# A decoder step on one Trainium2 core: the second feed-forward's gate/up tiles as seven block products in place of eight

## The reference

```
h = x + 1/2 * SwiGLU(RMSNorm(x))                    (feed-forward 1, D_FF = 2816)
n = RMSNorm(h); P = n @ w_in                        (u, q, k, v, index q/k/w, two gates)
h = h + (sigmoid(gs) * S5(u) + sigmoid(ga) * DSA(q, k, v)) @ w_out
h = h + 1/2 * SwiGLU(RMSNorm(h))                    (feed-forward 2)
y = RMSNorm(h)

def _swiglu(x, w_in, w_out):
    gate, up = jnp.split(x @ w_in, 2, axis=-1)
    return (jax.nn.silu(gate) * up) @ w_out
```

## Time and profile before

| | us |
|---|---|
| runs of the kernel before | 1451.26, 1454.88, 1445.98; median 1451.26 |
| the profiled execution, its span | 1450.0 |
| PE busy | 1376.6 (95%) |
| DVE, ACT, POOL busy | 654.6, 495.6, 265.2 |
| feed-forward 1, about | 24 to 430 |
| mixer, about | 432 to 1033 |
| feed-forward 2 and the end, about | 1033 to 1450 |

### The profile page before, as it was taken

One profiled execution on the slowest core, in us unless ns is written; L12 is line 12 of the kernel. 1 busy time (PEld: TensorE's weight loads), 2 busy tenths in 40 slices (PEclk: granted clock), 3 DMA queues, 4 the chain that ended last, 5 costly groups with the idle time before them and its releaser, 6 DMA issues.

```text
span 1450.0 us, 28752 instructions
## 1 busy us (share of the span) xinstructions
PE 1376.6 (95%) x11422; PEld 1289.9 (89%) x11422; DVE 654.6 (45%) x1093; ACT 495.6 (34%) x720; POOL 265.2 (18%) x325
## 2 busy tenths in 40 slices
PE   6999999999999899997999888899999999999996
PEld 5999999999987678875999777689999999999996
DVE  4333333434352226975987423245533443343344
ACT  5332222212232221244877432332432222222234
POOL 4000000288205002022667422100000000000000
PEclk9999999999997999999999999999999999999998
DMA  9522232333234363234222669663233322233221
GB/s 135 154 82 87 80 89 87 90 90 89 66 108 67 81 88 98 49 109 77 73 59 85 216 213 348 200 209 88 73 102 87 87 88 87 87 87 88 80 66 62
DMA packets 228818, 152.62 MB, mean 105 GB/s; under 512 B 27425, under 2 KB 209833, under 8 KB 228730
## 3 DMA queue, kind: packets, MB, share of 16 engines
q1 hardware_dynamic: 200512, 121.07, 28.9%
q0 software_dynamic: 7728, 19.97, 5.6%
q10 hardware_dynamic: 20490, 10.36, 3.3%
HBM read 141.85 MB, written 8.34 MB: 104 GB/s over the span
## 4 chain that ended last, share of the span: by engine, by line
PE 90%; DVE 3%; ACT 3%; issue 2%; DMA 1%; SPq 1%; ACTq 0%; DVEq 0%
PE ps L642 58%; PE ps L622 9%; PE ps L1036 3%; PE ps L1052 3%; PE ps L1153 3%; PE ps L1122 2%; PE ps L1205 1%; DVE uv L2139 1%; PE ps L1184 1%; PE ps L819 1%; PE ps L1067 1%; PE ps L926 1%; PE ps L1076 1%; PE ps L922 1%; PE ps L807 0%
## 5 line engine op out<-in xcount | busy, mean ns | idle before, releaser
L1778 DVE TENSOR_TENSOR w_low<-wraw,w_high 128x1024 fp32r<-128x1024 f32 x144 | 179.5, 1247 | 319.1 <-ACT w_high L1268 319.1
L1268 ACT ACTIVATE w_high<-wraw 128x1024 fp32r<-128x1024 f32 x144 | 152.6, 1060 | 443.3 <-PE ps L642 438.8
L642 PE MATMUL ps<-hn_high,w_high 128*128 128x272 f32 x1408 | 292.1, 289 | 2.9 <-DVE w_low L1778 2.9
L642 PE MATMUL ps<-hn_high,w_low 128*128 128x272 f32 x1408 | 291.9, 289 | 0.0
L642 PE MATMUL ps<-hn_low,w_high 128*128 128x272 f32 x1408 | 290.7, 288 | 0.0
L642 PEld LDWEIGHTS ps<-hn_high,w_high 128*128 128x128 f32 x1408 | 222.2, 189 | 3.1 <-issue 3.0
L642 PEld LDWEIGHTS ps<-hn_low,w_high 128*128 128x128 f32 x1408 | 221.8, 189 | 0.0
L642 PEld LDWEIGHTS ps<-hn_high,w_low 128*128 128x128 f32 x1408 | 220.2, 189 | 0.0
L642 PE MATMUL ps<-act_high,w_high 128*128 128x272 f32 x832 | 173.1, 289 | 3.4 <-DVE act_low L1778 1.9
L642 PE MATMUL ps<-act_high,w_low 128*128 128x272 f32 x832 | 172.0, 288 | 0.0
L642 PE MATMUL ps<-act_low,w_high 128*128 128x272 f32 x832 | 171.7, 288 | 0.0
(11 more groups left out here) (364 smaller groups left out, 1801.0 us busy)
## 6 DMA issues: line engine op xcount, KB each, us to landing
wraw<-in_w_ffn_in SPq DMA_DIRECT2D x88, 512.0 KB, 3.9
wraw<-in_w_ffn_out SPq DMA_DIRECT2D x32, 512.0 KB, 3.8
wslot<-in_w_in SPq DMA_DIRECT2D x16, 512.0 KB, 3.8
wraw<-in_w_ffn_out SPq DMA_DIRECT2D x16, 384.0 KB, 3.4
wslot<-in_w_in SPq DMA_DIRECT2D x4, 1024.0 KB, 5.6
wslot<-in_w_s_glu SPq DMA_DIRECT2D x16, 256.0 KB, 3.0
biasmem<-in_cache_k SPq DMA_DIRECT2D x16, 256.0 KB, 4.4
biasmem<-in_cache_k POOLq DMA_DIRECT2D x16, 256.0 KB, 5.1
```

Source lines behind the costliest of these rows:

```text
L642: ins = pe.matmul(ps[:, bank + h, 0:HALF], a[:, w_at, k, :], x[:, lo_at(k) if x is x_lo else k, h * HALF:(h + 1) * HALF], start=(k == 0 an ...
L1268: act_e.activation(wh[:, j % 2, :, :], wraw[:, j, :, :], ACT.Copy).then_inc(s["hi_done"], 1)
L1778: return dve.tensor_tensor(o, a, b, op)
```

## The change

For hidden tile f, write the gate tile's weights as two blocks of 512 input rows, G0 and G1, the up tile's as L0 and L1 ("lift"), and the scaled activations as X with upper and lower 512 channels and left and right token halves. Gate and up for both halves are 4 results of 2 blocks each, 8 block products. The change forms them from 7 products (the Winograd form of Strassen's scheme), each of 4 blocks x 3 pairs x one half = 12 matmuls, 84 a tile:

- **Weight sums.** Four of the seven left operands are sums of the blocks: L0+L1, L0+L1+G0, G0+L0, L0+L1+G0+G1 (signs sit in the activations and in the combining). They are formed in a DRAM scratch scr_w by POOL: plain copies, then transfers with accum_op=add. 22 tiles x 4 sums, 4 copies and 4 accumulates each of 256 KB, in 24 rounds; in each, copies, a wait for all, accumulates, a wait for all. Rounds 0 to 10 come behind the second unit of feed-forward 1, rounds 11 to 18 hold the 17 products for the S5 matrices between their transfers, rounds 19 to 23 come behind the clearing of uch, ahead of the page loads.
- **Activations.** hn_high and hn_low are replaced by xc_high and xc_low, 7 x [128, 4, 272]: three are quarters of X, one a difference, three sums made by cross_sums on DVE. scaled, block_high, cross_high run on ACT, block_low, cross_low on DVE.
- **PE.** `product` does 12 matmuls, with both passes of the high weights first and the low weights' pass behind a wait of its own. Seven products of a tile use four banks; products 4, 5, 6 add onto banks 0, 1, 3 after these were read. Tiles alternate between two sets of banks.
- **Combining.** ACT copies bank 0 to mid; DVE forms u, v, the right half of up, the two gate halves (the right one in two steps) and the left half of up, seven operations of 272 columns, then the gating product as before.
- **Splits.** Weights are split in pairs of products: three of 1024 columns and one of 512 a tile. Raw weights alternate between wraw (odd tiles) and a new wfront (even tiles); SP loads seven pieces of 256 KB a tile, released two tiles ahead.
- SP waits for all the sums (sums_in) and for the attention's matmuls before the first loads of feed-forward 2. The squares of the norms get other places. Feed-forward 1 is as before.

```diff
+            def product(f, p, high_ready, low_ready, block_wait=None):
+                pe.wait_ge(s["hi_done"], high_ready)
+                for n in range(3):
+                    a, x = ((high_slot(p), xc_high), (high_slot(p), xc_low), (low_slot(p), xc_high))[n]
+                    if n == 2:
+                        pe.wait_ge(s["lo_done"], low_ready)
+                    for k in range(4):
+                        if block_wait is not None and n < 2:
+                            block_wait(n, k)
+                        ins = pe.matmul(bank_of(f, p), a[:, k, :], x[:, XC[p], k, :], start=(n == 0 and k == 0 and p < 4),
...
+            def fused_tile(g, f, r=None):
...
+                for p in range(7):
...
+                    if p == 4:
+                        pe.wait_ge(s["first_out"], at(f + 1, 1))
...
+                    if p == 5:
+                        pe.wait_ge(s["combined"], at(combined_at(f, "v"), 7))
+                    if p == 6:
+                        pe.wait_ge(s["combined"], at(combined_at(f, "up1"), 7))
...
+            def cross_sums(j):
+                dve.wait_ge(s["x_scaled"], X0 + j + 1)
+                if j < 4:
+                    tt(xdiff[:, j, :], side(xs_block(j), 0), side(xs_block(j), 1), ALU.subtract).then_inc(s["cross_done"], 1)
+                    return
+                c = cross(j - 4)
+                dve.wait_ge(s["cross_done"], j - 3)
+                link(tt(c[:, 0, :], side(xs_block(j), 1), xdiff[:, j - 4, :], ALU.add))
+                tt(c[:, 1, :], side(xs_block(j - 4), 1), side(xs_block(j), 1), ALU.subtract)
+                tt(c[:, 2, :], side(xs_block(j), 0), c[:, 0, :], ALU.subtract).then_inc(s["cross_done"], 1)
...
+            def combine(g, f):
+                dve.wait_ge(s["unit_done"], product_at(g, f, 2))
+                dve.wait_ge(s["first_out"], f + 1)
+                tt(mid[:, 1, :], bank_of(f, 2), mid[:, 0, :], ALU.subtract).then_inc(s["combined"], 1)
+                dve.wait_ge(s["combined"], combined_at(f, "u"))
+                tt(mid[:, 2, :], mid[:, 1, :], bank_of(f, 1), ALU.subtract).then_inc(s["combined"], 1)
...
+                    for f in range(f0, f0 + m):
+                        if f > f0:
+                            combine_up0(g, f - 1)
+                            gate2(f - 1)
+                            tile_low_pair(g, f, 2)
+                            hidden_low(f - 1, f - 1 - f0)
+                            tile_low_pair(g, f, 3)
+                        if f < f0 + m - 1:
+                            tile_low_pair(g, f + 1, 0)
...
+                        combine(g, f)
+                        combine_up1(g, f)
+                        if f < f0 + m - 1:
+                            tile_low_pair(g, f + 1, 1)
...
+                        if f == 0:
+                            root_inverse(2)
+                        combine_gate(g, f)
```

DVE behind the units of `@ w_out`:

```diff
-                scaled_low(i)
+                if i in (6, 7):
+                    tile_low_pair(0, 0, i - 4)
                 if i:
+                    cross_sums(i - 1)
+                    block_low(i - 1)
+                    if i >= 2:
+                        cross_low(i - 2)
                     add_square(2, i - 1)
+            tile_low_pair(0, 0, 0)
+            cross_sums(DK - 1)
+            block_low(DK - 1)
+            cross_low(DK - 2)
+            tile_low_pair(0, 0, 1)
+            cross_low(DK - 1)
             add_square(2, DK - 1)
```

POOL:

```diff
+            def sum_copies(c):
+                if c < FK:
+                    pool.dma_start(scr_w[0, c], lift(0, c)).then_inc(s["sums_in"], 16)
+                    pool.dma_start(scr_w[2, c], gate(0, c)).then_inc(s["sums_in"], 16)
+                if 1 <= c <= FK:
+                    pool.dma_start(scr_w[1, c - 1], scr_w[0, c - 1]).then_inc(s["sums_in"], 16)
+                if c >= 2:
+                    pool.dma_start(scr_w[3, c - 2], scr_w[1, c - 2]).then_inc(s["sums_in"], 16)
+            def sum_adds(c):
+                if c < FK:
+                    pool.dma_start(scr_w[0, c], lift(1, c), accum_op=ALU.add).then_inc(s["sums_in"], 16)
+                    pool.dma_start(scr_w[2, c], lift(0, c), accum_op=ALU.add).then_inc(s["sums_in"], 16)
...
+            pool.wait_ge(s["unit_done"], 2)
...
+            ROUNDS, EARLY, LATE = FK + 2, 11, 19
...
+            for c in range(EARLY):
+                sum_copies(c)
+                sums_landed(c, 0)
+                sum_adds(c)
+                sums_landed(c, 1)
             pool.wait_ge(s["s5_scalars"], 2)
             pool.wait_ge(s["early_act"], 1)
+            for c in range(EARLY, LATE):
+                sum_copies(c)
+                lag_product(c - EARLY, 2 * (c - EARLY))
+                sums_landed(c, 0)
+                sum_adds(c)
+                if c == EARLY:
+                    lag_product(8, 1)
+                else:
+                    step_product(c - EARLY - 1, 2 * (c - EARLY) + 1)
+                sums_landed(c, 1)
+            step_product(7, 16)
             pool.sem_inc(s["prep_done"], 1)
...
+            for c in range(LATE, ROUNDS):
+                sum_copies(c)
+                sums_landed(c, 0)
+                sum_adds(c)
+                sums_landed(c, 1)
```

More of the change, by code:

```diff
@@ L414, in ffn_plan @@
                 u, tl, g_ = u + 2 * m, tl + m, g_ + m
-                yield "out", f0, m, u, tl, FK * which + g_
+                yield "out", f0, m, u, tl, g_
                 u, tl = u + DK, tl + DK
-        def in_parts(which, f0, m):
-            if which == 0:
-                return [(i, i + 1) for i in range(m // 2)]
-            return [(0, 1), (1, m // 2)] if f0 == 0 else [(0, m // 2)]
+        U1 = FFN_UNITS + DK
+        X0 = 5
+        XC = (0, 1, 4, 5, 2, 3, 6)
+        BANK = (0, 1, 2, 3, 0, 1, 3)
@@ new lines, in f_group, with split_at, out_split_at, product_at @@
+        def f_group(f):
+            return sum(f >= f0 for f0, _ in GROUPS) - 1
+        def split_at(g, f, q):
+            if f > GROUPS[g][0]:
+                return U1 + 4 * f + DK * g + q + 1
+            if g == 0:
+                return U1 + (q + 2) % 4 + 1
+            return U1 + 4 * f + DK * g + (q + 3 if q < 2 else q - 2 - DK + 3)
+        def out_split_at(g, j):
+            return U1 + 4 * sum(GROUPS[g]) + DK * g + j + 1 + (2 if g < 2 and j >= 2 else 0)
+        def product_at(g, f, p):
+            return U1 + 7 * f + DK * g + p + 1
@@ new lines, in out_done_at, with gated_at, out_added_at, combined_at @@
+        def out_done_at(g, j):
+            return U1 + 7 * sum(GROUPS[g]) + DK * g + j + 1
+        def gated_at(f):
+            return FE0 + FFN_TILES + DK + f + DK * f_group(f) + 1
+        def out_added_at(g, j):
+            return FE0 + FFN_TILES + DK + sum(GROUPS[g]) + DK * g + j + 1
+        COMBINED = ("u", "v", "up1", "gate0", "gate1", "gate1_scaled", "up0")
+        def combined_at(f, what):
+            return 7 * f + COMBINED.index(what) + 1
+        def pair_bytes(q):
+            return 32 if q < 3 else 16
@@ L715, in ffn @@
                                     pe.wait_ge(s["ffn_ev"], i * 2 + (t0 + j // 2 + FE0 - 1))
-                                unit(j % 2, hnh, hnl, DK, 4 * (j // 2) + 2 * (j % 2), norm_block if which == 0 and f0 == 0 and j == 0 else None)
+                                unit(j % 2, hnh, hnl, DK, 4 * (j // 2) + 2 * (j % 2), norm_block if f0 == 0 and j == 0 else None)
                     else:
@@ new lines, in first_blocks, with body, out_unit2 @@
+            def first_blocks(p):
+                def body(n, k):
+                    ready = (block_at(k), cross_at(k), cross_at(k + 4), cross_at(k + 4), block_at(k + 4), block_at(k + 4), cross_at(k + 4))[p]
+                    pe.wait_ge(s["xn_low" if n else "xn_high"], ready)
+                return body
+            def out_unit2(g, f0, m, j):
+                pe.wait_ge(s["lo_done"], FE0 + out_split_at(g, j))
+                if j < 2:
+                    pe.wait_ge(s["combined"], combined_at(f0 + m - 2 + j, "up0"))
+                else:
+                    pe.wait_ge(s["out_scaled"], DK * g + j - 1)
+                hidden = last_hidden(m, FE0 + FK + f0 + m)
+                for k in range(m):
+                    if j == 0:
+                        hidden(k)
+                    for n in range(3):
+                        a, x = ((wh[:, j % 2, :, :], acth), (wh[:, j % 2, :, :], actl), (wl[:, j % 2, :, :], acth))[n]
+                        for h in range(2):
+                            ins = pe.matmul(ps[:, 4 * (j % 2) + h, 0:HALF], a[:, k, :], side(x[:, k, :], h),
+                                            start=(k == 0 and n == 0), stop=(k == m - 1 and n == 2), skip_group_check=True)
+                ins.then_inc(s["unit_done"], 1)
@@ new lines, in ffn2 @@
+            def ffn2():
+                for g, (f0, m) in enumerate(GROUPS):
+                    for f in range(f0, f0 + 2):
+                        fused_tile(g, f)
+                    with pe.Fori(1, m // 2) as r:
```

(13 more changed lines are left out.)

476 lines of the change are left out of this document (349 added, 127 removed).

## The result

The changed kernel takes 1472.95 us (median of 4 runs, 1464.93 to 1476.89), the kernel before beside it 1453.07: a ratio of 1.014, interval 1.010 to 1.018. It is slower by 1.4%, and outside the predicted range of 1421 to 1468. The profiled executions have spans of 1472.7 and 1450.0: 22.7 us to explain, and with the 33.1 us that the products were to save, 56 us of new cost.

The account below looks back on a forecast made before the run. PE was taken as the bound, busy 95% of a 1450.0 us span. 1450.0 - 33.1 (products) + 8.5 (start) + 0 (sums) + 4 (exchange) = 1429.4, with 1.3 for the median about 1430; own range 1421 to 1438, all told 1421 to 1468.

Parts of the forecast that it names:

- Products, -33.1: Second feed-forward's gate/up tiles on PE: 84 matmuls in place of 96, 22 tiles x 12 x 0.1253 us, 33.1 us gone.
- rival D: Gate/up tiles: 84 matmuls with a new moving operand each take as long as 96, no gain, 1463 us; chance 0.03.
- Steady tile, 0: Gate/up tile of 10.52 us: DVE's 8.8 us and ACT's 5.6 hide under the products, PE never waits; cost zero.
- Sums on POOL, 0: Weight-sum rounds on POOL's queue: S5 products done at 433.3, before PE needs prep_done at 436.1; cost 0.
- R = 18.5: Length in us of one POOL round of four copies and four accumulates, bounds 8.7 and 46.
- rival A: POOL's rounds take 19 to 22 us, prep_done up to 25 us late; 1447 us, range 1432 to 1455; chance 0.19.
- Start of the feed-forward, +8.5: Second feed-forward's start: PE stalls 5.5, 2.4 and about 2.1 us for DVE's work; 8.5 us lost, bounds 0 and 12.
- Exchange of u, +4: Exchange of u through DRAM, beside POOL's last five rounds, takes a fifth more: 4 us, ends 0 and 12.
- Weight loads of feed-forward 1, 0: First feed-forward's weight loads, issued three units (18 us) ahead at 33% DMA share, lose nothing beside the rounds: 0.
- The slower rival (B): POOL's rounds over 22.6 us delay prep_done; at 24 it is 61 us late, 1491 us; chance 0.16.

Follow-up runs that it names:

- e1: Changed kernel with PE's wait for an even tile's first weight pair, in the tile loop, set to that pair's own split count; 1460.41 us, ratio 1.006.
- e3: Changed kernel without the eight rounds between the S5 products, five late rounds kept, summed pieces read from one weight block; 1441.34 us, ratio 0.996.
- e6: Changed kernel, count corrected, rounds spread: 0-10 as before, none between S5 products, 11-12 after prep_done, 13-17 after clearing uch, 18-23 after page loads; 1434.24 us.
- e10: As e6, but rounds 13 to 23 wait for the second unit of the output projection and later tile loads wait for their rounds; 1427.80 us, ratio 0.983.
- e4: Changed kernel with every accumulating transfer made a plain copy of the same bytes, order and waits unchanged; span 1447.1, one execution, 1448.79 us.
- e8: e6 with DVE's work at the second feed-forward's start reordered: pair 0's split before pair 3's, last blocks' squares behind the low parts; 1432.43 us, ratio 0.987.
- e7: Changed kernel, count corrected, with POOL adding the weight sums in SBUF during the second feed-forward, no sum through DRAM; 1442.75 us, ratio 0.994.

## Why the prediction was wrong

**Products, -33.1: right.** 22 x 12 matmuls at 0.1255 to 0.1257 us; rival D is out.

**Steady tile, 0: wrong, +13.9 us.** The failing step is "Nothing waits on PE's side; the least margin is 1.2 us". I laid the tile out by what each product reads, and took for granted that its wait names that. The wait names a count, and the count was off by two in every even tile. By the data the layout was right: with the count corrected no wait is left (e1), and DVE's 66.6 us over eight tiles are 8.3 a tile, where I had 8.8. This could have been computed from the diff: for an even tile of the loop the count is that of pair 2, which DVE forms behind the gating product.

**Sums on POOL, 0: wrong, +27.7 us.** The step is R = 18.5: it was 21.4 to 22.2, where the text had priced 8 us for each us over 18.9. The term that was mis-sized is the accumulate's half: 10.3 us in the sum (3.2 issue, 5.1 landing, 2 for the second read), 13.8 in the mean of eight rounds. Of it 12.6 is the half without a pause and 1.2 what the pauses add; the copies' half came to 7.6 instead of 8.3. The pauses stood in no step, and in the eight rounds that decide they weigh more: R was 22.2 there, 19.9 without them. The mechanism was rival A's (rounds of 19 to 22 us, prep_done up to 25 late), just past its upper end, and I had given it 0.19. At the measured R its formula gives the end of the last product to a microsecond, with some luck: POOL began 2.4 us later and the last product took 3.9 us, not 5.5. A fast total needed R at its breakpoint or below, and I had set my forecast 0.4 us from that edge with bounds of 8.7 and 46: the chances should have been near even.

The Trainium skill, DMA: Bandwidth & Descriptors, "Anatomy of one DMA — SWDGE (gpsimd) path", would make a single 256 KB transfer 2.6 us, an estimate from its fit, and a round some 12. The trace disagrees and decides: with four in flight it is 5 to 7 us from the last copy's issue to POOL's next step, and about 11 for accumulates without a pause.

**Start of the feed-forward, +8.5: nearly right, 9.6 measured**, with other parts: 5.1 (for 5.5) at pair 0, counted from start to start, then 1.7 in all where I had 2.4 and 2.1, and 2.5 of a lower clock that stood in no step. That the sum came out near is luck.

**Exchange of u, +4: right, 4.1.** e3 shows it too (22.7 us), e6 with 21.2 in part, e10 that it goes when none runs there.

**Weight loads of feed-forward 1, 0: wrong, but hidden.** Its matmuls ended 6 us late in the changed kernel (436.0, before 430.1) and PE reached the wait for POOL 9.7 late. In e4, where POOL was in time, the transposes came 8.2 late, so a smaller R would not have brought this part to 0. Only a part of it is traced, to DVE's split beside POOL's product (e4, above). In e3, e6 and e10, where no round runs between the products, the norm's matmuls came 1.3 to 1.5 late.

**The slower rival (B)** asked for R over 22.6; it did not come to that. The kernel was slower because A and the even tiles came together, 27.7 + 13.9 against 33.1 (the start's 9.6 and the mixer's 5.8 lie near the 8.5 and 4 of the forecast), a case that no rival held.

What stays open: the cause of POOL's pauses, the rest of the late end of the first feed-forward, and how much of the 3.7 us by which e10 comes later to the attention's output weights (956.01, before 952.27) is the sums; its executions differ by 9 us among themselves.

## What to carry to other kernels

Before you call a wait harmless, work out the count it waits for and which instruction brings it, above all in loops whose first round has another order: data that is ready early does not help. Put work on a shared queue only behind the last thing that someone waits for: eight rounds ahead of prep_done cost 27.7 us, eleven beside the second feed-forward, whose loads are asked for two tiles ahead, under 1 us. And when a price is missing from the trace and the answer turns within 2% of your estimate, give both sides the same chance.

## What the hardware showed beyond that

- An accumulating DRAM-to-DRAM transfer of 256 KB with rows of 512 B is 516 packets where a copy is 68, and four of them land some 11 us after the last issue where copies land in 5 to 7. Long rows bring two thirds of the difference between rounds back, pauses counted.
- POOL paused 3.9 to 5.7 us in the middle of issuing, with no wait that the profile shows, nine times in the first 19 rounds (42.5 us together); with plain copies three times, with long rows twice. The places are regular: before the third accumulate of rounds 3, 6, 9, 12, 15 and 18 and before the second of rounds 5, 10 and 15. e1 has the same nine, the profiles of e3, e6, e8 and e10 the same five before 280, and with plain copies the three before the second of 5, 10 and 15 stay. So a pause seems to follow what was issued before it, and not what runs beside it; what it waits for is not shown.

```profile
310.53 1.71 POOL L1987 DMA_DIRECT2D scr_w<-in_w_ffn_in  x1
317.41 1.14 POOL L1989 DMA_DIRECT2D scr_w<-in_w_ffn_in  x1 [5.17 <-issue]
...
379.91 1.16 POOL L1987 DMA_DIRECT2D scr_w<-in_w_ffn_in  x1 [4.42 <-issue]
...
385.82 1.14 POOL L1989 DMA_DIRECT2D scr_w<-in_w_ffn_in  x1 [4.75 <-issue]
...
451.02 1.14 POOL L1989 DMA_DIRECT2D scr_w<-in_w_ffn_in  x1 [4.96 <-issue]
```

And two of the three with plain copies:

```profile
128.19 0.72 POOL L1987 DMA_DIRECT2D scr_w<-in_w_ffn_in  x1 [4.56 <-issue]
...
210.29 0.72 POOL L1987 DMA_DIRECT2D scr_w<-in_w_ffn_in  x1 [3.52 <-issue]
```

- A DVE split of 1024 columns took 1.9 times as long beside POOL's adds (2.31 for 1.22 us, e7). Operations of 272 columns that read PSUM kept their 0.43 us there, while one on SBUF alone went from 0.44 to 1.07.
- A DMA share of 1.11 over 66 us went with a PE that never waited.
- TensorE's granted clock fell to its lower level after a stand of 4.92 us (0.51 over the 5.56 us behind it) and also after four short stands within 10 us (0.50 over 3.80 us).
